# Gate and output products of a hybrid encoder layer with seven block products for eight, and what has to be turned for it

## What is computed

```python
h = _rmsnorm(x, norm1[l])
proj = jnp.einsum('bsd,de->bse', h, w_in[l])       # the last 3 * 2048 columns: gate_logits (touched)
...
g = jax.nn.sigmoid(gate_logits.astype(jnp.float32)).reshape(B, S, N_BRANCH, D).astype(x.dtype)
merged = (g[:, :, 0] * jnp.einsum('bsp,pd->bsd', a, w_pool_out[l])
          + g[:, :, 1] * jnp.einsum('bsp,pd->bsd', bconv, w_conv_out[l])
          + g[:, :, 2] * jnp.einsum('bsp,pd->bsd', c, w_attn_out[l]))
x = x + jnp.einsum('bsd,de->bse', merged, w_o[l])  # touched
h2 = _rmsnorm(x, norm2[l])
f = jnp.square(jax.nn.relu(jnp.einsum('bsd,df->bsf', h2, w_ff1[l])))
x = x + jnp.einsum('bsf,fd->bsd', f, w_ff2[l])
```

## Time and profile before

| | |
|---|---|
| time, median of 3 runs | 2784.98 us (2784.83 to 2785.03) |
| profiled execution | 2781.99 us, its span 2780.2 us |
| mean granted TensorE clock | 0.994 |
| PE busy | 2730.7 us, 98% of the span |
| DVE, ACT busy | 1700.1 us (61%), 1134.7 us (41%) |
| moved by DMA | 422.53 MB, mean 152 GB/s |
| gate stage on PE | from 605.66 to 1301.97 us |
| w_o on PE | from 1301.97 to 1481.4 us |

### The profile page before, as it was taken

One profiled execution on the slowest core, in us unless ns is written; L12 is line 12 of the kernel. 1 busy time (PEld: TensorE's weight loads), 2 busy tenths in 40 slices (PEclk: granted clock), 3 DMA queues, 4 the chain that ended last, 5 costly groups with the idle time before them and its releaser, 6 DMA issues.

```text
span 2780.2 us, 38256 instructions
## 1 busy us (share of the span) xinstructions
PE 2730.7 (98%) x14934; PEld 2363.6 (85%) x14934; DVE 1700.1 (61%) x2197; ACT 1134.7 (41%) x1604; POOL 37.2 (1%) x28
## 2 busy tenths in 40 slices
PE   7999999999999999999999999999999899999998
PEld 5688998778888888888888999999999688888887
DVE  8565524543333333334247988888886788888787
ACT  5422333333233232323245665666565333333332
POOL 4000000000000000000000000000000000000000
PEclk9999999999999999999999999999999999999999
DMA  4333222223333333333532556655668767575843
GB/s 136 101 91 98 84 84 69 75 71 97 98 97 96 94 98 98 93 97 125 191 114 91 188 176 220 208 169 193 213 200 317 255 227 287 197 287 159 322 150 111
DMA packets 295097, 422.53 MB, mean 152 GB/s; under 512 B 15728, under 2 KB 192496, under 8 KB 294960
## 3 DMA queue, kind: packets, MB, share of 16 engines
q1 hardware_dynamic: 279648, 361.80, 40.6%
q10 hardware_dynamic: 15312, 58.85, 5.6%
HBM read 353.36 MB, written 67.11 MB: 151 GB/s over the span
## 4 chain that ended last, share of the span: by engine, by line
PE 90%; DVE 4%; DMA 4%; issue 1%; ACT 1%; SPq 0%; ACTq 0%; DVEq 0%
PE main L362 13%; PE main L364 13%; PE main L363 13%; PE main L881 7%; PE main L880 7%; PE main L879 7%; PE aux L928 3%; PE aux L929 3%; PE aux L930 3%; DMA group<-w_ff 3%; PE main L928 3%; PE main L929 3%; PE main L930 3%; PE main L720 1%; PE main L721 1%; PE main L722 1%
## 5 line engine op out<-in xcount | busy, mean ns | idle before, releaser
L339 DVE TENSOR_TENSOR w_lo<-w_raw,w_hi 128x512 fp32r<-128x512 f32 (+1 forms) x504 | 350.4, 698 | 768.7 <-ACT w_hi L332 765.3
L332 ACT ACTIVATE w_hi<-w_raw 128x512 fp32r<-128x512 f32 (+1 forms) x504 | 314.3, 626 | 814.9 <-PE main L364 637.7
L362 PE MATMUL main<-act_hi,w_hi 128*128 128x512 f32 (+1 forms) x1296 | 511.5, 395 | 4.2 <-DVE w_lo L339 4.2
L364 PE MATMUL main<-act_hi,w_lo 128*128 128x512 f32 (+1 forms) x1296 | 504.9, 390 | 0.0
L363 PE MATMUL main<-act_lo,w_hi 128*128 128x512 f32 (+1 forms) x1296 | 504.4, 389 | 0.0
L879 PE MATMUL main<-sf,f_wh 128*128 128x256 f32 x1728 | 489.9, 284 | 4.3 <-ACT keeps L1243 3.1
L880 PE MATMUL main<-sf,f_wh 128*128 128x256 f32 x1728 | 489.7, 283 | 0.0
L881 PE MATMUL main<-sf,f_wl 128*128 128x256 f32 x1728 | 489.7, 283 | 0.0
L879 PEld LDWEIGHTS main<-sf,f_wh 128*128 128x128 f32 x1728 | 332.4, 192 | 4.7 <-ACT keeps L1243 3.3
L880 PEld LDWEIGHTS main<-sf,f_wh 128*128 128x128 f32 x1728 | 332.5, 192 | 0.0
L881 PEld LDWEIGHTS main<-sf,f_wl 128*128 128x128 f32 x1728 | 332.5, 192 | 0.0
(11 more groups left out here) (217 smaller groups left out, 4230.0 us busy)
## 6 DMA issues: line engine op xcount, KB each, us to landing
w_raw<-w_in SPq DMA_DIRECT2D x184, 512.0 KB, 3.6
group<-w_ff SPq DMA_DIRECT2D x160, 512.0 KB, 5.0
f1raw<-w_ff SPq DMA_DIRECT2D x126, 512.0 KB, 6.0
sf<-f_dram ACTq DMA_DIRECT2D x56, 1024.0 KB, 13.4
f_dram<-piece_hi SPq DMA_DIRECT2D x112, 256.0 KB, 4.4
f_dram<-piece_lo SPq DMA_DIRECT2D x112, 256.0 KB, 5.3
w_raw<-w_o SPq DMA_DIRECT2D x32, 512.0 KB, 3.8
w_raw<-w_attn_out SPq DMA_DIRECT2D x16, 512.0 KB, 3.3
```

Of the source, the lines that this page charges most:

```text
L332: act.activation(w_hi[:, j % SLOTS, :, 0:width], w_raw[:, (j // 2) % RAWS, UK * (j % 2):UK * (j % 2) + UK, 0:width], ACT.Copy).then_inc(hi ...
L339: dve.tensor_tensor(w_lo[:, j % SLOTS, :, 0:width], w_raw[:, (j // 2) % RAWS, UK * (j % 2):UK * (j % 2) + UK, 0:width], w_hi[:, j % SLOTS, ...
L362: pe.matmul(out, wh, hi[:, kt, :], start=(kt == last_kt[0]), stop=False)
L364: mm = pe.matmul(out, wl, hi[:, kt, :], start=False, stop=(kt == last_kt[1]))
```

## The change

The gate logits are made in six phases J = 0 to 5, and w_o in two, J = 6 and 7, each of 28 granules of 12 matmuls as in f2 (`granule(J, n, g)`: product n of seven, fourth g of the contraction). That makes 6 x 28 x 12 = 2016 matmuls for the gates' 2304 and 672 for w_o's 768. The order of the seven products differs by phase: `FIRST_G` for J = 0, `FIRST_W` for J = 6, `NORMAL` for the others. Tokens are on the partitions now.

What comes with it: `h` (2048 x 512, kept in `xin`) is written to DRAM early, its room is used by the attention, and it is loaded back; eight mixes and eight subtractions make the operands of products 1 to 4 (`mix_gs`, `hi_gs`, `lo_gs`). Results of the seven products are copied out of the accumulators by ACT (`copy_gate`) and added by DVE (`add_gate`), go through the sigmoid in place, and are written to DRAM (`spill_gate`). The branch activations are written to DRAM as well. A branch stage of its own, 64 units of 12 matmuls, makes the three projections; per branch and block of 512 columns a gate block of 1 MB is loaded (`load_sig`) and `merge(s)` multiplies and adds. The merged m has tokens on the partitions: PE turns it (`turn_m`, four times 16 transposes), ACT copies it back (`turned_m`), and its operands are mixed and split for w_o (`mix_m`, `hi_m`, `lo_m`). x comes back for the residual in two halves (`load_x_back`), `add_w` adds w_o's products to it, and x2 is written to DRAM in four parts (`spill_x2`). In the MLP buffers move, and `cf` is mixed in place with its spills a few granules later; its products stay. The weight loads of the gates and of w_o come in the same `load_group` as f2's, and the splits no longer go on across the border into the gate stage (`if n + PREFETCH < 6 * UP`).

```diff
+        FIRST_G = ([(n, g) for g in range(4) for n in (0, 5)] + [(1, g) for g in range(4)] +
+                   [(n, g) for g in range(4) for n in (4, 3, 2)] + [(6, g) for g in range(4)])
+        FIRST_W = ([(n, g) for gs in ((0, 1), (2, 3)) for ns in ((0, 1), (4, 5)) for g in gs for n in ns] +
+                   [(n, g) for g in range(4) for n in (3, 2)] + [(6, g) for g in range(4)])
...
+            spill_c(7)
+            spill_b(2)
+            sp.wait_ge(pv_mm, ATTN_HEADS)
+            for h in range(2):
+                for kk in range(2):
+                    k0 = 8 * kk + 4 * h
+                    sp.dma_start(xin[:, k0:k0 + 4, :], h_dram[k0:k0 + 4].rearrange("k p c -> p k c")
+                                 ).then_inc(h_back[h], 16)
+                if h == 0:
+                    sp.wait_ge(unit_done, u_g)
+                    load_group(2)
+            for G in range(3, G_BASE[6]):
+                load_group(G)
+
...
+            sp.wait_ge(m_mixed, 8)
+            sp.wait_ge(m_lo, 14)
+            load_x_back(0)
+            for r in range(7, 10):
+                load_group(G_BASE[6] + r)
...
+            sp.wait_ge(y_added, 9)
+            spill_x2(0, 0)
+            spill_x2(0, 1)
+            for G in range(G_BASE[7] + 2, G_BASE[8]):
+                load_group(G)
...
-                        for n in range(UP if gate else units):
-                            g = i * G_U + (u_g + j)
-                            if gate:
-                                unit(pe, g, j, 2 * n, H, 2 * (p % 2), act_hi, act_lo)
...
+                    if n == 2:
+                        pe.wait_ge(gate_copied, 3 * J + 1)
+                    if n == 3:
+                        pe.wait_ge(gate_copied, 3 * J + 2)
...
+                        sh, sl = operand(J, n, 0, kt, t), operand(J, n, 1, kt, t)
+                        part = bank[:, b0 + t, :]
+                        first = n in (0, 1, 4, 5) and g == 0 and e == 0
+                        last = g == 3 and e == 1
+                        pe.matmul(part, sh, wh, start=first, stop=False, skip_group_check=True)
+                        pe.matmul(part, sh, wl, start=False, stop=False, skip_group_check=True)
+                        mm = pe.matmul(part, sl, wh, start=False, stop=last, skip_group_check=True)
...
-                        for m in range(2):
-                            act.activation(sg[:, m], main[:, 2 * parity + m, :], ACT.Sigmoid).then_inc(sig_done, 1)
...
+            def copy_gate(J, i):
+
+                n = (0, 1, 2)[i]
...
+                b0 = (0, 2, 0)[i]
+                act.activation(gb[J % 2][(0, 3, 2)[i]][:], aux[:, b0:b0 + 2, :], ACT.Copy).then_inc(gate_copied, 1)
...
+                if idx == 11 and J:
+                    copy_gate(J, 0)
+                if idx == 12 and J:
+                    copy_gate(J, 1)
...
+                if n + PREFETCH < 6 * UP:
+                    split_lo(dve, u_att + n + PREFETCH, n + PREFETCH)
...
+            def mix_t1(J, g):
+                b11, b12 = landed(J, place_of(J, 0, g)), landed(J, first_12(J, g))
...
+                dve.tensor_tensor(tx_at(J)[g][:], b12, b11, ALU.subtract).then_inc(t_done, 1)
...
+            def mix_gs(n, h):
+
+                a11, a12, a21, a22 = h_block(0, 0, h), h_block(1, 0, h), h_block(0, 1, h), h_block(1, 1, h)
+                if n == 1:
+                    dve.wait_ge(h_back[h], 32)
+                    ins = dve.tensor_tensor(a22, a21, a22, ALU.add)
...
+            def lo_gs(n, h):
+
+                dve.wait_ge(gs_hi, gs_at(n, h))
+                dve.tensor_tensor(gs_part(n, h, 1), gs_source(n, h), gs_part(n, h, 0).bitcast(F32),
+                                  ALU.subtract).then_inc(gs_lo, 1)
...
+            mix_t1(0, 0)
+            for g in range(4):
+                lo2(0, 0, g)
+                if g < 3:
+                    mix_t1(0, g + 1)
+                if g == 2:
...
+                    dest = sig[s % 2][:, t, :] if b else mt[:, t, c0:c0 + S]
+                    dve.tensor_tensor(dest, bank[:, t, :], sig[s % 2][:, t, :], ALU.mult).then_inc(gate_mul, 1)
...
+                if g == u_w - 1:
+                    mix_t1(6, 0)
+                    lo2(6, 0, 0)
+                    lo2(6, 1, 0)
+                if kt in (3, 7, 15):
```

More of the change, by code:

```diff
@@ L131, in build @@
         probT = at("probT", [P, PCOLS], F32, M + 26 * KB)
[L132 to L138, removed]
@@ new lines, in _ @@
+            load_b(u_b + 4)
+            load_b(u_b + 6)
+            load_branch(3, 12, 16)
+            load_sig(0)
+            load_sig(1)
+            next_sig = 2
+            for g in range(u_b + 8, u_w, 2):
+                load_b(g)
+                while next_sig < 12 and 4 * next_sig + 4 * (next_sig // 3) <= (g - u_b - 8):
+                    load_sig(next_sig)
+                    next_sig += 1
+            load_group(G_BASE[6])
+            while next_sig < 12:
+                load_sig(next_sig)
+                next_sig += 1
@@ L833, in _ @@
+                    pe.matmul(bank[:, t, :], th, b_hi4[:, g % SLOTS], start=first, stop=False)
+                    pe.matmul(bank[:, t, :], th, b_lo4[:, g % SLOTS], start=False, stop=False)
+                    mm = pe.matmul(bank[:, t, :], tl, b_hi4[:, g % SLOTS], start=False, stop=last)
                 mm.then_inc(unit_done, 1)
-                if i and kt == 4:
-                    turn_x2(i - 1, main if i % 2 == 0 else aux)
+            for n, g in order_of(6):
+                granule(6, n, g)
+                if (n, g) == (1, 0):
+                    pe.wait_ge(gate_mul, 48)
+                    pe.wait_ge(m_added, 32)
+                    turn_m(3, main)
@@ new lines, in _ @@
+            mix_t1(6, 3)
+            lo2(6, 1, 2)
+            lo_m(5, 1)
+            lo2(6, 0, 3)
+            lo_m(3, 1)
+            mix_t3(6, 2)
+            lo2(6, 1, 3)
+            mix_t3(6, 3)
+            lo2(6, 4, 2)
+            lo2(6, 5, 2)
+            lo2(6, 4, 3)
+            mix_t2(6, 0)
+            lo2(6, 5, 3)
+            for g in range(4):
+                lo2(6, 3, g)
+                if g < 3:
+                    mix_t2(6, g + 1)
+                if g == 0:
+                    add_w(6, 0)
+                    add_w(6, 1)
+                lo2(6, 2, g)
+                mix_t4(6, g)
+                if g == 1:
+                    add_w(6, 2)
+                if g == 2:
+                    add_w(6, 3)
@@ new lines, in _ @@
+            for g in range(4):
+                if g == 1:
+                    add_w(7, 0)
+                    add_w(7, 1)
+                lo2(7, 4, g)
+                mix_t2(7, g)
+                if g == 3:
+                    lo_h2(0, 0)
+                lo2(7, 3, g)
+                if g < 3:
+                    mix_t3(7, g + 1)
+                else:
+                    mix_t4(7, 0)
+                if g == 2:
+                    lo_h2(6, 0)
+                    mix_h2(1, 0)
+                lo2(7, 2, g)
@@ L1883, in dve_after @@
                         add_c(q, 1)
+            mix1(0, 0, 0)
+            lo1(0, 0, 0)
+            lo_h2(3, 0)
+            lo1(0, 1, 0)
+            add_w(7, 7)
+            add_w(7, 8)
             mix1(0, 1, 0)
```

1536 lines of the change are left out of this document (1010 added, 526 removed).

## The result

The changed kernel takes 2813.05 us (median of 4, 2809.33 to 2818.50) against 2785.01; the ratio is 1.0105, 95% interval 1.0092 to 1.0118. Its profiled execution took 2815.88 us with a span of 2814.1, so the comparison of the two traces is one of +33.9 us, and that of the medians one of +28.0. The forecast was 2794.5, the range 2756 to 2815; two of the four executions lie above its end.

A forecast was written before the change was run, and what follows sets the result against it. PE was taken to bound the kernel (busy 98%). -80.0 + 29.9 + 18.8 + 3 + 20.7 + 16.1 + 1 = +9.5 us on 2782.0 gave 2791.5, plus 3.0 for the median: 2794.5; range 2756 to 2815.

The forecast's parts named there:

- rival D: J = 0 and J = 6: holes follow closely, half-clock spells join; 12 to 20 us more, about 2810; chance 0.18.
- The saving: Gates lose 288 matmuls (65.3 us), w_o 96 (21.8), transposes add 7.0; unbroken PE needs 80.0 us less.
- The start of J = 0: Gates' first granules: PE waits 5.3 us for DVE, then 10.4 at granule 1 for group 2 behind h, plus 3.3 of clock.
- The term of 29.9: All J = 0 losses: 5.3 + 10.4 + 3.3 + 6.7 + 2.5 + 1.7 us; range 22 to 35.
- Phases 1 to 5: Granule 9 waits 2.3 us for ACT's copy, plus 1.4 of clock, in each of five phases: 18.8 us (5 to 25).
- rival B: J = 1 to 5: copy fits before granule 9, or the clock stays up; 2776 to 2787 us; chance 0.13.
- J = 6: w_o's first half: DVE lags, group 7 lands late behind x loads, granule 12 waits 8.0 us; 20.7 in all (12 to 26).
- J = 7: w_o's second half: third group behind x2 writes 6.0 + 3.3, addition 1.0, turning 4.1 + 1.7; 16.1 us (8 to 20).
- The branch stage: The three projections: DVE's splits and merges fit within PE's time, sigmoid loads hidden; +3 us (0 to 8).
- f1: Start of the MLP's f1: 1 us more; the MLP's matmuls and its two slow places stay.
- Rival A: J = 0, 6, 7: bulk ahead in SP's queue doesn't delay groups; 34 us less, about 2760; chance 0.15.
- C: Whole change: the saving comes through, phases run like f2, only DVE's start costs 10 us; 2715; chance 0.06.

The follow-up runs named there:

- the doubled run: Against the kernel combining the earlier edits (2765.3 us): h's loads each followed by an equal DRAM copy, second-half m sums cut to 64 columns; 2770.8 us, ratio 0.9960.
- the last version: Changed kernel with the runs' edits except later x2 turning, plus copies ahead of two h operands (J = 0), an addition ahead of a lo (J = 7); 2760.95 us.

## Why the prediction held, and where its sizes were off

The direction and the cause held: a saving of 80 us, eaten by holes at the places named. The number held only just. The measured 2813.05 lies 18.6 above the forecast and 2 below the end of the range, and not in the band of the forecast itself (2783 to 2805) but in that of rival D (2805 to 2825), though D's mechanism explains only a part of it. The terms missed by +12.0 in J = 0, +18.5 in J = 7 and +2.9 ahead of the gates, and by -5.5 in J = 1 to 5, -2 in the branches and -1.4 in f1; that these last three were too large is luck, and it kept the number inside the range. (These are differences of the profiled executions, +24.3 in all. The changed kernel's lies 2.8 above its median and the forecast had added 3.0, which leaves the 18.6.)

**The saving** was right: the phases without a hole take 76.2 us (the run with earlier copies), 28 x 12 x 0.2267, and the balance closes with holes and the clock alone. **The start of J = 0** was right in mechanism and size: 5.2 us for 5.3, a wait of 9.8 (10.4 forecast) at granule 1 behind a group issued behind h, and the doubled run confirms what sets it. The term of 29.9 left out two things. One is the wait at granule 24, 4.5 us and its clock (5.5 in the run that removed it): the sum has ACT's copies behind products 0 and 1 and not the third, which `FIRST_G` puts directly ahead of the granule that needs ACT next. The other is the clock behind the very first wait, which the sum charged with nothing. Windows of granule 0 and of granule 24:

```profile
613.90:618.92 5.02, 4.97 (x12) 3.64 (x12) 0.00 (x0) 0.00 (x0) 0.00 (x0) 0.58 1.01 300
712.46:717.50 5.04, 4.98 (x12) 3.93 (x13) 4.54 (x5) 1.60 (x2) 0.00 (x0) 0.54 0.00 0
```

Each took 5.0 us for 2.7, at a granted clock of 0.58 and 0.54. Granule 13 waited 3.9 for 2.5, granule 5 6.0 for 5. **Phases 1 to 5** were right in cause, and too large in size: 2.06 us for 2.3, and the clock, for which I took 1.4 each, fell behind one of the five. So rival B was void in its first half, as all five holes were there, and right in its second for four of them.

**J = 6** came out at 20.5 for 20.7, and this is agreement in the sum more than in the cause. The step "only then SP issues four loads of x, and behind them group 7" names the load that landed last, but taking it away gave 4.1 of 11.3 us: the buffer of group 7 was freed by a DVE mix that was itself late. DVE has 77 us of work in 98, and three buffers allow one group in flight behind another. How the 16 us that J = 6 still loses in the last version divide between DVE's queue and the buffers is not settled; a fourth buffer wasn't tried.

**J = 7** is the term that failed: 34.6 us for 16.1. The third group's wait was there (5.5 for 6.0, and 7.1 back when removed), and the turning behind granule 23 waited 5.4 for 4.1. Missing were the four places at which ACT takes the turned x2 in front of a hi: the sum has no term for them. There ACT waits in a strict queue for PE, which cost it its lead over PE and 13.6 us. **The branch stage** (1.0 for 3) and **f1** (-0.4 for 1) were as forecast. The 2.9 us ahead of the gates I had not looked for: a wait of 1.25 us at 97.9 us for ACT, which stood 8.40 us for a raw weight tile that SP loads behind the four writes of h (11.5 us each to landing), and a slower start (a clock of 0.83 from 20 to 40 us for 0.86). The start differs from run to run: the convolution ends at 606.6 to 608.7. None of this was tested.

So the gain of 80 us went into 114 of waits and clock. 51 of them were shown by taking their cause away: 13.3 and 5.5 behind ACT's copies, 13.6 behind its turned x2, 7.1 and 4.1 where transfers stood in front of a group, and 7.5 by the order of SP and of DVE's lo's together in J = 0. The others, above all the late start of J = 0 and what is left in J = 6, were read from the traces and not removed. Rival A was refuted, by the doubled run in J = 0 and by the removed writes in J = 7; C was out; rival D, the clock that stays down, was partly in it: 28 us in three phases, where the sum has about 16. Of these 12 us more, 4.6 are the first granule and granule 24 of J = 0, places that the sum gave no clock. On what the two halves of the change are worth: gates and branches took 692.6 us for 696.3, w_o 214.5 for 179.4. In the last version they are 664.8 and 188.8; seven products for w_o still cost more than eight did. That making m's and x2's operands beside them is the reason is argued from DVE's queue; the one test of it, 4 us less of DVE, gave 1.9.

## What to carry to other kernels

A product of fewer matmuls pays only where the engines that feed it keep their lead. Count, at each start of a stage and at each odd instruction in ACT's or DVE's queue, how many granules of lead are left, not how busy the engine is: ACT was busy 46% of J = 7 and cost it 13.6 us. Removing the transfer that lands last shows whether it was the cause or only the last of several: here it gave 7.1 of 8 us in one place and 4.1 of 11 in another. Where the same bytes must land before the same granule, reordering them moves the hole.

## What the runs showed of the hardware

The clock doesn't answer to the length of a wait alone. PE waited 2.06 us ahead of granule 9 in each of J = 1 to 5; windows behind that of J = 1 and that of J = 2 in the changed kernel:

```profile
754.00:756.00 2.00, 2.00 (x8) 1.58 (x7) 0.74 (x1) 0.00 (x0) 0.00 (x0) 0.67 0.56 127
756.00:758.00 2.00, 2.00 (x6) 1.52 (x6) 0.00 (x0) 0.32 (x1) 0.00 (x0) 0.50 1.03 394
...
834.00:836.00 2.00, 2.00 (x10) 1.65 (x9) 0.87 (x1) 0.00 (x0) 0.00 (x0) 1.00 0.53 111
836.00:838.00 2.00, 2.00 (x11) 1.65 (x10) 0.41 (x1) 1.06 (x1) 0.00 (x0) 1.00 1.02 391
```

Behind the first the clock fell to 0.50 (1.2 GHz for 2.4), behind the second it did not. J = 1 took 80.1 us in four of the traces that have this wait, among them the changed kernel's, and 78.5 or 78.6 in two others. The same gap costs 2.4 or 4.0 us. The Trainium skill, "TensorE: Matmul & The Clock Gate", HAM oscillation, says that the engine is throttled again behind idle gaps and pays half of the throttled time; the half is what the earlier trace rows and these rows show, and the traces add that one and the same gap may or may not do it.

A wider spread of the changed kernel is not shown. Its four executions lie within 9.2 us and the first four of the kernel before within 1.6, but ten later ones of the kernel before lie within 6.9, and four with group 7 first within 4.3.
